# q and k by 32x32 squares, sums in pairs, norm folds on VectorE, x by halves

## The reference, cut to what matters

```python
# first stack, both layers: norm of the gated Mamba output in SSM_GROUPS = 2 groups of 512
y_ssm = y_ssm * jax.nn.silu(z)
y_ssm = rms_norm(y_ssm, ssm_norm_w)             # mean of squares over a group

# second stack: conditioning, a (1024) x (1024 x 6144) product for each of four layers
shift1, scale1, gate1, shift2, scale2, gate2 = jnp.split(jax.nn.silu(c) @ ada_w[i] + ada_b[i], 6)

# mLSTM (third layer of the second stack): q, k and v by blocks of 4 channels
xc = jax.nn.silu(causal_dwconv(xm, conv_w, conv_b))
q, k, v = headwise(xc, w_q), headwise(xc, w_k), headwise(xm, w_v)   # 4x4 blocks on the diagonal
...
mu, var = jnp.mean(hc), jnp.mean(jnp.square(hc - mu))               # over a head of 512
hc = (hc - mu) * lax.rsqrt(var + LN_EPS)
```

## Time and profile before

| | |
|---|---|
| median of three runs | 2500.68 us (2498.67 to 2503.42) |
| profiled execution | 2501.5 us, span of its trace 2498.8 us |
| TensorE busy | 2481.0 us, 99% of the span |
| DVE busy | 1333.2 us, 53% |
| ScalarE busy | 551.4 us, 22% |
| DMA | 457.93 MB, mean 183 GB/s |

### The profile page before, as it was taken

The page is one execution under the profiler, slowest core; times in us unless marked ns, Lnnn a source line. Parts: engine busy times, 40 slices in busy tenths (PEclk is TensorE's granted clock), DMA queues, the critical chain, the costliest instruction groups (busy, mean ns, idle before and its releaser), DMA issues.

```text
span 2498.8 us, 34814 instructions
## 1 busy us (share of the span) xinstructions
PE 2481.0 (99%) x14484; PEld 2167.2 (87%) x14484; DVE 1333.2 (53%) x3157; ACT 551.4 (22%) x1084; POOL 167.5 (7%) x268
## 2 busy tenths in 40 slices
PE   9999999999999999999999999999999999999998
PEld 7879888987888898988898988898889889889888
DVE  6652674565268637598454579752535332325332
ACT  3451100144200022311041311023412111432101
POOL 2000110000031000011000121030000000000000
PEclk9999999999999999999999999999999999999999
DMA  7935886574489755588554488643244444334442
GB/s 209 235 102 183 290 288 213 141 192 106 121 289 315 242 161 149 202 303 294 177 154 134 141 308 295 233 148 100 87 141 146 152 154 149 118 116 160 154 153 76
DMA packets 403240, 457.93 MB, mean 183 GB/s; under 512 B 50751, under 2 KB 374776, under 8 KB 403084
## 3 DMA queue, kind: packets, MB, share of 16 engines
q1 hardware_dynamic: 370098, 340.53, 43.6%
q0 software_dynamic: 29936, 112.73, 12.5%
q10 hardware_dynamic: 3050, 2.46, 0.4%
HBM read 451.48 MB, written 1.29 MB: 181 GB/s over the span
## 4 chain that ended last, share of the span: by engine, by line
PE 95%; DVE 3%; DMA 1%; issue 0%; ACT 0%; DVEq 0%; SPq 0%; POOLq 0%; ACTq 0%
PE job_bank L892 68%; PE job_bank L947 11%; PE mix_bank L947 4%; PE job_bank L1288 3%; DVE sb_arena L2557 1%; PE mix_bank L1235 1%; PE job_bank L1263 1%; PE mix_bank L1199 1%; PE mix_bank L1534 1%; PE mix_bank L1249 1%; DVE sb_arena L2531 1%; PE mix_bank L923 1%; PE mix_bank L1578 0%; PE mix_bank L1356 0%; DMA sb_arena<-row_scratch 0%
## 5 line engine op out<-in xcount | busy, mean ns | idle before, releaser
L892 PE MATMUL job_bank<-sb_h,sb_ring 128*128 128x256 f32 (+1 forms) x5920 | 1301.6, 380 | 0.0
L892 PEld LDWEIGHTS job_bank<-sb_h,sb_ring 128*128 128x128 f32 (+1 forms) x5920 | 1116.1, 190 | 169.2 <-issue 17.1
L892 PE MATMUL job_bank<-sb_arena,sb_ring 128*128 128x256 f32 x1840 | 401.3, 380 | 0.0
L892 PEld LDWEIGHTS job_bank<-sb_arena,sb_ring 128*128 128x128 f32 x1840 | 348.6, 190 | 51.1 <-issue 3.5
L2531 DVE SCALAR_TENSOR_TENSOR sb_arena<-sb_arena,sb_par 128x256 f32<-128x256 f32 x722 | 333.9, 502 | 13.3
L2557 DVE SCALAR_TENSOR_TENSOR sb_arena<-sb_arena,sb_c_act 128x256 f32<-128x256 f32 x672 | 325.9, 485 | 24.0
L1736 ACT ACTIVATE sb_arena<-job_bank 128x512 f32<-128x512 f32 x178 | 106.2, 597 | 1025.6 <-PE job_bank L892 968.5
L947 PE MATMUL job_bank<-sb_h,sb_ring 128*128 128x128 f32 x1600 | 184.1, 275 | 1.4 <-ACT sb_h L2028 1.4
L947 PEld LDWEIGHTS job_bank<-sb_h,sb_ring 128*128 128x128 f32 x1600 | 181.2, 192 | 1.8 <-issue 1.6
L833 POOL DMA_DIRECT2D sb_arena<-in_ada_w x96 | 85.0, 887 | 842.6 <-DVE sb_arena L2557 530.6
L2529 DVE TENSOR_SCALAR sb_arena<-sb_arena,sb_par 128x256 f32<-128x256 f32 x263 | 97.0, 411 | 78.5 <-ACT sb_arena L1736 78.4
(11 more groups left out here) (451 smaller groups left out, 1721.5 us busy)
## 6 DMA issues: line engine op xcount, KB each, us to landing
sb_arena<-in_ada_w POOLq DMA_DIRECT2D x96, 1024.0 KB, 7.7
sb_ring<-in_ffn_w_up SPq DMA_DIRECT2D x88, 1024.0 KB, 5.1
sb_ring<-in_w_up SPq DMA_DIRECT2D x44, 1024.0 KB, 7.5
sb_ring<-in_ffn_w_down SPq DMA_DIRECT2D x32, 1024.0 KB, 5.0
sb_ring<-in_w_in SPq DMA_DIRECT2D x24, 1024.0 KB, 5.8
sb_ring<-in_w_down SPq DMA_DIRECT2D x16, 1024.0 KB, 6.0
sb_ring<-in_hg_w_in SPq DMA_DIRECT2D x16, 1024.0 KB, 5.5
sb_ring<-in_ml_w_up SPq DMA_DIRECT2D x16, 1024.0 KB, 5.5
```

The costliest lines, as they stand in the source:

```text
L892: mm = pe.matmul(o, st, mv, start=(k0 + k == 0 and t == 0), stop=(k0 + k == kn - 1), skip_group_check=True)
```

## The change

- **Pairs of quads.** The six quads of a layer stand behind jobs 11 and 19 and down job 1, two at each. ADA_PARTS goes from 8 to 10.
- **Squares.** q and k use only the 32x32 squares on the diagonal of `ml_bd`. Tile t, strip g of the input goes to output strip (g + t) % 4 of bank `M[1 + t]`; q lies in the first half of both banks, k in the second. 16 matmuls of 32x32 take the place of four. Both banks are signalled when k is done, and the block waits for all three copies of the pair before. ScalarE's copies write q and k of a tile at once.
- **Folds.** `gated_sums` and `head_sums` are gone. DVE adds the four tiles in two steps, 4 to 2 and 2 to 1, and the statistics take a full block of ones. For the heads, squares go to `ml_k`, so that one operation folds values and squares. The fills around become 7 (9 in the last head) and 5.
- **Halves.** All eight tiles of the first half of x are transposed, then those of the second; the spreading follows, each half waiting for its own diagonal; DVE waits for it with `x_turned` 6.

```diff
-ADA_PARTS = 8
+ADA_PARTS = 10
...
+        ml_xc, ml_qk, ml_v = ml(IT, T), ml(2, IT, T), ml(NT, INNER)
+        ml_q, ml_k = ml_qk[:, 0, :, :], ml_qk[:, 1, :, :]
...
+        ml_fold = t1[:, 0:4, :].rearrange("p (r k) t -> p r k t", r=2)
...
                 def condition(n):
-                    if cond and n in (7, 11, 15, 19):
+                    if cond and n in (11, 19):
+                        ada_quad()
                         ada_quad()
...
                 def conditioning(i):
-                    if i < 2:
+                    if i == 1:
+                        ada_quad()
                         ada_quad()
...
-            turn_x(0)
-            turn_x(1)
-            pe.wait_ge(s.rstd_tok, 3)
             for j in range(NT):
+                pe.wait_ge(s.x_in[j], 16)
+                for k in range(KD):
+                    mm = pe.transpose(quad(M[k // 2])[:, k % 2 * 2 + j, :], x_tok[:, j, k * P:(k + 1) * P], ident[:, :])
+                    if j == NT - 1 and k % 2:
+                        mm.then_inc(s.x_turned, 1)
+            for j in range(NT):
+                pe.wait_ge(s.rstd_tok, 2 + j)
                 mm = pe.matmul(L[2][:, j * P:(j + 1) * P], ones[:, :], rs_diag[:, j, :], start=True, stop=True)
             mm.then_inc(s.x_turned, 1)
-            turn_x(2)
-            turn_x(3)
...
-                def gated_sums(g):
+                def gated_stats(g):
...
                     j = out1[g][0]
...
                     pe.wait_ge(bank_read[j % 4], j // 4)
...
                     pe.wait_ge(s.gpart_ready, GROUPS * l + g + 1)
-                    pe.matmul(L[out1[g][0] % 4][:, T:2 * T], pick[:, 2, :], red[:, g * T:(g + 1) * T], start=True,
+                    pe.matmul(L[j % 4][:, T:2 * T], ones[:, :], red[:, g * T:(g + 1) * T], start=True,
...
-                gated_sums(0)
-                gated_sums(1)
...
                 pe.wait_ge(s.xbc_act, CT * L1 + m + 2)
+                if n:
+                    pe.wait_ge(s.mq_read, 3 * n)
                 for i in range(2):
-                    if n:
-                        pe.wait_ge(s.mq_read, 3 * n - 1 + i)
                     for t in range(2):
-                        mm = pe.matmul(pair(M[1 + i])[:, t, :], ml_bd[:, i, m + t, :], ml_xc[:, m + t, :], start=True,
-                                       stop=True)
-                    mm.then_inc(s.mq_ready, 1)
+                        for g in range(4):
+                            at, to = 32 * g, 32 * ((g + t) % 4)
+                            mm = pe.matmul(M[1 + t][to:to + 32, i * T:(i + 1) * T], ml_bd[at:at + 32, i, m + t, at:at + 32],
+                                           ml_xc[at:at + 32, m + t, :], start=True, stop=True, skip_group_check=True)
+                        if i:
+                            mm.then_inc(s.mq_ready, 1)
...
-                fill(beside, 5 if i + 1 < ML_HEADS else 7)
-                head_sums(i)
-                fill(beside, 2)
+                fill(beside, 7 if i + 1 < ML_HEADS else 9)
                 head_stats(i)
                 fill(beside, 5)
...
-                vec.wait_ge(s.x_turned, 4)
+                vec.wait_ge(s.x_turned, 6)
...
                 def keep_sums(g):
-                    vec.wait_ge(s.gsum_ready, GROUPS * l + g + 1)
-                    vec.tensor_copy(red[:, g * T:(g + 1) * T], L[plan[("out1", l)][g][0] % 4][:, 0:T]).then_inc(s.gpart_ready, 1)
+                    vec.wait_ge(s.gsq_ready, GROUPS * l + g + 1)
+                    v = xbc[:, 4 * g:4 * g + 2, :]
+                    step(vec.tensor_tensor(v, v, xbc[:, 4 * g + 2:4 * g + 4, :], ALU.add))
+                    settle()
+                    vec.tensor_tensor(red[:, g * T:(g + 1) * T], xbc[:, 4 * g, :], xbc[:, 4 * g + 1, :], ALU.add)\
+                       .then_inc(s.gpart_ready, 1)
...
-                vec.wait_ge(s.hcol_sum, i + 1)
-                vec.tensor_copy(red[:, :], M[2][:, :]).then_inc(s.hpart_ready, 1)
+                vec.wait_ge(s.hsqr_ready, i + 1)
+                step(vec.tensor_tensor(ml_fold, ml_qk[:, :, 4 * i:4 * i + 2, :], ml_qk[:, :, 4 * i + 2:4 * i + 4, :],
+                                       ALU.add))
+                settle()
+                vec.tensor_tensor(red[:, :].rearrange("p (r t) -> p r t", r=2), ml_fold[:, :, 0, :],
+                                  ml_fold[:, :, 1, :], ALU.add).then_inc(s.hpart_ready, 1)
```

More of the change, by code:

```diff
@@ L231, in __init__ @@
         self.mo_ready = sem("mo_ready")
-        self.hcol_sum = sem("hcol_sum")
         self.hpart_ready = sem("hpart_ready")
@@ L1602, in ml_values @@
                 mm.then_inc(s.mn_ready, 1)
-            def head_sums(i):
-                pe.wait_ge(s.hsqr_ready, i + 1)
-                for r, src in ((0, ml_q[:, 4 * i:4 * i + 4, :]), (T, ml_sq)):
-                    for k in range(4):
-                        mm = pe.matmul(M[2][32 * k:32 * k + 32, r:r + T], ones[:, 0:32], src[:, k, :], start=True,
-                                       stop=True)
-                mm.then_inc(s.hcol_sum, 1)
             def head_stats(i):
@@ L1616, in head_stats @@
                 for r in (0, T):
-                    mm = pe.matmul(M[3][:, r:r + T], pick[:, 2, :], red[:, r:r + T], start=True, stop=True)
+                    mm = pe.matmul(M[3][:, r:r + T], ones[:, :], red[:, r:r + T], start=True, stop=True)
                 mm.then_inc(s.hstat_ready, 1)
@@ L1826, in _ @@
             act.activation(first_w, L[1][:, 0:KD], ACT.Copy).then_inc(s.x_ready, 1)
-            for b, turned in enumerate((2, 3, 5, 6)):
-                act.wait_ge(s.x_turned, turned)
+            for b in range(4):
+                act.wait_ge(s.x_turned, 2 + b)
                 act.activation(x[:, 2 * b:2 * b + 2, :], pair(M[b]), ACT.Copy).then_inc(s.x_ready, 1)
@@ L2085, in keep_pair @@
                 m = 2 * n
-                for i, dst in enumerate((ml_v[:, :, m * P:(m + 2) * P], ml_q[:, m:m + 2, :], ml_k[:, m:m + 2, :])):
+                for i, dst in enumerate((ml_v[:, :, m * P:(m + 2) * P], ml_qk[:, :, m, :], ml_qk[:, :, m + 1, :])):
                     act.wait_ge(s.mq_ready, 3 * n + i + 1)
```

19 lines of the change are left out of this document (2 added, 17 removed).

## The result

The changed kernel took **2483.7 us** (median of five runs, 2483.35 to 2485.22) beside 2500.68 us of the kernel before: ratio 0.9933, 95% interval [0.9919, 0.9946]. That is 3.3 us less than the forecast of 2487.0 and 0.3 us under the low end of its range. Two later series of the same kernel gave 2485.92 us (0.9938 [0.9926, 0.9950]) and 2485.35 us (0.9938 [0.9924, 0.9951]). Beside the kernel before on the same chips these are 15.3 and 15.4 us less, where the first series gives 17.0, and a ratio of 0.9938 is 2485.2 us by the first series' measure, inside the range. A part of the 3.3 us is therefore scatter between executions, and the experiments show of what kind.

The account below looks back on a forecast made before the run. TensorE, busy 99% of the span, was taken as the bound. Savings of 3.2 + 5.5 + 3.1 + 1.1 + 0.75 = 13.7 us from 2500.7 gave 2487.0 us, range 2484 to 2494.

Parts of the forecast that it names:

- What bounds the kernel: Whole kernel: TensorE busy 99% of the span, so a pass that goes saves its spacing unless TensorE must wait.
- Squares: q and k matmuls: eight 32x32 tiles run at once, 1.23 us a block instead of 1.94; 5.5 us saved.
- Rival 1: q and k squares run only four at a time, 2.07 us a block; total 2493.6 us; chance 0.12.
- Rival 2: q and k: row strips can't write one bank together, two squares at once, 3.80 us a block; 2507.4 us; chance 0.09.
- Rival 3: Waits at last-stage conditioning sums, heads, start and square blocks take more of the gain; 2490.6 us; chance 0.09.
- rival 4: Whole kernel: the weight stream sets the time and takes the gain back; 2500.7 us; chance 0.02.
- Gated norm: Norm sums of the gated values: narrow sums go four times at 0.77 us, DVE's adds hidden; 3.1 us saved.
- Conditioning sums: Ada quads in four GLU stages: 24 quads become 12 pairs, 0.34 us each, less one wait; 3.2 us saved.
- TensorE waits the 0.77 us that it came sooner: Fourth GLU stage: DVE's late unit ends unchanged, so TensorE waits 0.77 us, cutting 4.0 to 3.2 us.
- Heads: Heads' norm sums: DVE's adds make TensorE wait; 0.40 us gained in three heads, 0.1 lost in the last; 1.1 us.
- Start: x transposed by halves: first weight matmul at 10.78 us instead of 11.78; 0.75 us gained, ends 0 and 1.1.
- if that change comes with the work, 1.0 us is gained; if at its own instant, 0.5: Start: two cases for TensorE's switch from 1.2 to 2.4 GHz, placed at 14.4 us; 0.75 us taken.

Follow-up runs that it names:

- four-corner kernel: Changed kernel with the squares of both channel tiles of a pair in the same four corners of the array (output strip = input strip); 2491.89 us, ratio 0.9961.
- after: The changed kernel itself in its first series, with its first profile; 2483.7 us, ratio 0.9933.
- after again: The changed kernel, unchanged, run again for a second profile; 2485.92 us, ratio 0.9938.
- gap and filler runs: Changed kernel with x's second eight transposes held back, 2488.16 us; kernel before with ten repeated transposes in TensorE's start waits, 2499.59 us.
- before again: The kernel before the change, unchanged, run again for a second profile; 2501.21 us, ratio 1.0002.
- squares-only: The kernel before with q and k by 32x32 squares alone, plus the waits and ScalarE copies that go with them; 2495.25 us, ratio 0.9975.

## Why the prediction was right or wrong

**What bounds the kernel** was right: a pass of TensorE that goes is worth its spacing. All parts but the start follow from counting passes and asking when DVE delivers.

**Squares**: right in mechanism and size. The block is 1.23 us as summed (0.20 + 0.67 + 0.05 + 0.31), 0.71 saved a pair, and 5.65 in all against 5.5. The 0.15 more comes from pair 6, where both kernels wait 0.41 us for ScalarE ahead of q and k: 0.90 is saved there. From the first pass of the block to the gates the squares need 1.03 us there and 1.02 in the other pairs, the whole tiles of before 1.92 and 1.82; and the 0.09 that the squares' way in costs more than theirs is spent in the wait. Rivals 1 and 2 fall. Rival 1 predicted 2.07 us a block, and forced by the four-corner kernel it measures 1694.68 - (1691.73 + 1.16 - 0.27) = 2.06: its price was right, its condition wrong. Rival 2 predicted 3.80. What the Trainium skill states (TensorEngine Tiling, Restrictions and Gotchas), on which rival 2 leaned, doesn't hold for this use of a bank: four row strips write disjoint partitions of one bank at once, 1.23 us a block where exclusion would give 3.80. That row and column tiling compose, as the Trainium skill says (TensorE: Matmul & The Clock Gate, Part 3), the trace bears out for eight tiles. Rival 3 falls too, since TensorE waited less than forecast at the quads and in the heads, and so does rival 4, since the gain was not taken back.

**Gated norm**: right, 3.07 against 3.1, and the cover is 3.0 us.

**Conditioning sums**: three stages at 1.00 us, right (3 x 0.34). The fourth brought 0.59 in place of 0.24. The step that failed is "TensorE waits the 0.77 us that it came sooner", for a wait of 1.1 us. It took the pair as one block that waits whole. But each quad has its own wait: the first one finds its units and runs, and its 0.46 us are taken from the 0.77. So the lateness costs 0.31 us more than before (1.08 - 0.46 = 0.62 between the quads, where the late single quad of before lost 0.32), and 0.09 us of it stand at a later weight pass. 1.00 - 0.31 - 0.09 is 0.60.

**Heads**: mechanism right, size off by 0.54 us. DVE's step from L3175 (now L3156) to the statistics was summed as 2.57 us (1803.33 to 1805.90) and is 2.35 (1786.76 to 1789.11). I put 0.04 ahead of each add. The first add reads nothing that the operation before it writes, the kernel puts no wait between the two, and it starts 0.35 behind that one's start, where I had 0.47: 0.12 less. From the last add's end to the statistics, 0.06 stands where I had 0.15: 0.09 less. Against that the four passes of the statistics take 1.13 from idle where they took 1.04. So 0.40 + 0.22 - 0.09 is 0.53 a head, measured 0.54. In the last head nothing instead of a loss of 0.1, by the same steps.

**Start**: the term that was mis-sized most, and the one that took the time out of the range. Forecast 0.75 with ends 0 and 1.1, measured 2.75 in the profile of after, 0.50 in its second profile, 1.9 on average over seven. The failed step is "if that change comes with the work, 1.0 us is gained; if at its own instant, 0.5". Both cases let the first weight passes run at 1.2 GHz, because I placed the clock's rise by the weight passes. I never asked what TensorE does before them. The 16 transposes are work too. In six of seven profiles the rise came before the first weight pass, and the slow passes that I had left in are gone (six of them, 0.21 each, 1.24 us by the drift). Where it came before the scales too, as in after, their matmuls are faster, so h's first tile is ready sooner (1.5 us up to the first pass, where I had 1.0). Where it came late, in after again, the forecast's own case for that held: 0.50 us, as written for a change "at its own instant". My upper end of 1.1 was no bound of the unknown cost, since it left this case out. The gap and filler runs show that it is the unbroken work, by whichever order, that makes the difference.

**Not in the sum**: 0.41 us at L1199, where the change alters nothing. It scatters, and that it fell on the good side in after was luck. The waits of before have "L1199 <- DVE sb_arena L2846: 0.3", those of before again have no such row, and squares-only has 0.7.

**The range** gave 1.3 us to noise. The changed kernel's 15 runs spread over 3.7 us, 2483.35 to 2487.05; the two at the ends were profiled, and differ at two places, the start and the depthwise stage. The time in the first series, 0.3 us under the range, is thus the start's gain and some luck: the later series lie inside it, still 1.6 us beyond the forecast's gain. With the start's average (1.2 over the forecast), the heads, the fourth stage and 0.15 at the squares (1.0) the sum comes to 2484.8; the 15 runs have a median of 2485.2.

## What to carry to other kernels

Take the waits out of TensorE's first microseconds before counting what the transposes there cost, and judge any change of the start by several profiles: the clock's rise moves by microseconds between executions of one program. The gain, some 2 us of 2500 here, shows in the traces and hardly in the times. Block-diagonal 32x32 work pays when its squares occupy different row and column strips at once; rotate the output strip so that two blocks share no corner. A step that hands sums from TensorE to another engine is worth its passes only as far as there are passes of others to put ahead of the result: count DVE's chain start to start, and move the fill until the wait is gone.

## What the runs showed of the hardware that I had not expected

- In the one profile with an idle stretch of 1.6 us between two runs of eight transposes the rise of TensorE's clock came at 17.7 us; with unbroken work it came at 7.2 to 10.2 us in ten of eleven profiles, and where it came by 7.3 us, transposes were all of that work. Work from 2.1 us on didn't bring it ahead of 7.2.
- Eight 32x32 tiles run at once, four row strips of them into one bank; on the first pair of after they start 0.0067 us apart.
- A stage of 512 narrow passes at some 0.03 us each stalls in 15 of 18 profiles, by 0.1 to 2.5 us in all, with no releaser in the trace, mainly at one place of TensorE's stream. The main stall ends 1.2 to 1.6 us after the end of a 16 KB transfer of the kind "instruction".
- DVE started an operation 0.08 us before the end of the one ahead of it where the kernel puts no wait between them (the heads' first add); where the kernel waits for the first one's end, 0.03 to 0.04 us lie between the two.
